# Cross attention's keys: one scaling pass, turned by VectorE squares and GpSimd DMAs; four small reorderings elsewhere

## The reference, cut to what matters

```
def memory_cross_attention(hn, mem, w_xq, w_xkv, g_mem, g_xq, g_xk, w_xo):
    q = (hn @ w_xq).reshape(B, T, 4, 256);  q = rmsnorm(q, g_xq)
    k, v = jnp.split(rmsnorm(mem, g_mem) @ w_xkv, 2, axis=-1)
    k = rmsnorm(k.reshape(B, M, 4, 256), g_xk)
    logits = jnp.einsum('bthd,bmhd->bhtm', q, k) * 256 ** -0.5
    p = jax.nn.softmax(logits, axis=-1)
    return jnp.einsum('bhtm,bmhd->bthd', p, v).reshape(B, T, 1024) @ w_xo
```

## Time and profile before

| | |
|---|---|
| median of three executions | 882.25 us |
| the profiled execution's own time | 883.71 us |
| its span, first to last instruction | 881.9 us |
| PE busy | 873.5 us (99%) |
| DVE busy | 601.1 us (68%) |
| ACT busy | 439.4 us (50%) |
| POOL busy | 183.2 us (21%) |
| mean granted TensorE clock | 0.998 |
| DMA | 154.67 MB, mean 175 GB/s |

### The profile page before, as it was taken

How to read it: one execution, slowest core, us unless ns; L and a number is a source line. 1 busy time by engine, 2 the same in 40 slices (tenths; PEclk the granted TensorE clock), 3 DMA queues, 4 the chain that set the end, 5 groups by cost and what they waited for, 6 DMA issues and landing times.

```text
span 881.9 us, 12721 instructions
## 1 busy us (share of the span) xinstructions
PE 873.5 (99%) x5023; PEld 751.7 (85%) x5023; DVE 601.1 (68%) x875; ACT 439.4 (50%) x613; POOL 183.2 (21%) x214
## 2 busy tenths in 40 slices
PE   9999999999999999999999999999999999999998
PEld 6897888888988999988888789888888888888886
DVE  5478988998696666745454948977785566665742
ACT  6365456864545555533344426546554544443531
POOL 0432234863110000000004222100100024444500
PEclk9999999999999999999999999999999999999999
DMA  8874542445146655655569765523542567775862
GB/s 297 200 258 144 191 144 87 132 129 166 48 139 195 193 191 190 190 191 191 190 212 258 201 165 192 189 98 118 170 142 79 164 199 218 219 220 160 254 218 72
DMA packets 87651, 154.67 MB, mean 175 GB/s; under 512 B 10528, under 2 KB 18512, under 8 KB 87472
## 3 DMA queue, kind: packets, MB, share of 16 engines
q1 hardware_dynamic: 80352, 144.55, 51.1%
q0 software_dynamic: 4720, 5.86, 3.7%
q10 hardware_dynamic: 2528, 3.56, 1.2%
HBM read 147.53 MB, written 1.44 MB: 169 GB/s over the span
## 4 chain that ended last, share of the span: by engine, by line
PE 92%; DVE 5%; DMA 1%; ACT 1%; issue 1%; SPq 0%; DVEq 0%; ACTq 0%
PE gemm L540 68%; PE gemm L1048 5%; PE mixbank L1048 5%; DVE w_lo L1872 2%; PE mixbank L603 1%; PE mixbank L702 1%; DMA raw<-in_w_in_dram 1%; PE mixbank L727 1%; PE mixbank L808 1%; PE mixbank L1213 1%; DVE mix L2010 1%; PE gemm L1241 1%; PE mixbank L713 1%; PE mixbank L750 1%; PE mixbank L902 0%
## 5 line engine op out<-in xcount | busy, mean ns | idle before, releaser
L1872 DVE TENSOR_TENSOR w_lo<-raw,w_hi 128x2048 fp32r<-128x2048 f32 (+3 forms) x132 | 288.0, 2189 | 180.3 <-ACT w_hi L1303 180.1
L1303 ACT ACTIVATE w_hi<-raw 128x2048 fp32r<-128x2048 f32 (+3 forms) x140 | 255.4, 1833 | 204.7 <-DMA raw<-in_w_in_dram 57.1
L540 PE MATMUL gemm<-w_hi,s_hi 128*128 128x512 f32 (+3 forms) x784 | 208.6, 386 | 0.6 <-ACT s_hi L1339 0.3
L540 PE MATMUL gemm<-w_lo,s_hi 128*128 128x512 f32 (+3 forms) x784 | 201.9, 378 | 1.2 <-DVE w_lo L1872 1.2
L540 PE MATMUL gemm<-w_hi,s_lo 128*128 128x512 f32 (+3 forms) x784 | 202.1, 378 | 0.0
L540 PEld LDWEIGHTS gemm<-w_lo,s_hi 128*128 128x128 f32 x784 | 142.6, 188 | 29.2 <-DVE w_lo L1872 2.1
L540 PEld LDWEIGHTS gemm<-w_hi,s_lo 128*128 128x128 f32 x784 | 143.2, 189 | 27.7
L540 PEld LDWEIGHTS gemm<-w_hi,s_hi 128*128 128x128 f32 x784 | 140.5, 189 | 26.0 <-issue 1.7
L2743 POOL TENSOR_TENSOR sm<-sm 128x2 f32<-128x2 f32 (+5 forms) x13 | 21.6, 1663 | 400.9 <-DVE sm L1933 296.5
L373 POOL DMA_DIRECT2D hid_moved<-hid_blocks x96 | 54.7, 578 | 72.4 <-DVE hid_blocks L2685 70.1
L2737 POOL TENSOR_TENSOR w_lo<-raw,w_hi 128x2048 fp32r<-128x2048 f32 x8 | 36.8, 4614 | 36.1 <-ACT w_hi L1303 36.1
(11 more groups left out here) (365 smaller groups left out, 1183.8 us busy)
## 6 DMA issues: line engine op xcount, KB each, us to landing
raw<-in_w_in_dram SPq DMA_DIRECT2D x40, 1024.0 KB, 5.2
raw<-in_w_mlp_up_dram SPq DMA_DIRECT2D x16, 1024.0 KB, 5.6
raw<-in_w_mlp_down_dram SPq DMA_DIRECT2D x16, 1024.0 KB, 5.1
raw<-in_w_gate_dram SPq DMA_DIRECT2D x10, 1024.0 KB, 5.3
raw<-in_w_up_dram SPq DMA_DIRECT2D x10, 1024.0 KB, 5.1
raw<-in_w_down_dram SPq DMA_DIRECT2D x10, 1024.0 KB, 5.4
raw<-in_w_out_dram SPq DMA_DIRECT2D x8, 1024.0 KB, 5.2
raw<-in_w_xkv_dram SPq DMA_DIRECT2D x8, 1024.0 KB, 5.1
```

What stands on the lines that cost most here:

```text
L540: return nc.tensor.matmul(G[b % 2][t][:, 0:width], lhs, rhs, start=kt == 0 and not (low_x or low_w), stop=kt == blk["kt"] - 1 and (low_x i ...
L1303: nc.scalar.activation(w_hi[:, n % SLOTS, 0:kn, 0:width], raw[:, n % SLOTS, 0:kn, 0:width], ACT.Copy)\
L1872: V.tensor_tensor(w_lo[:, s, 0:kn, 0:width], raw[:, s, 0:kn, 0:width], w_hi[:, s, 0:kn, 0:width].bitcast(F32), ALU.subtract)\
```

## The change

1. Keys. Each head's 256 columns are scaled by norm and gain in one instruction (`scalar_tensor_tensor`, 8 in all), placed between VectorE's two splits of block `B_XQ`. The keys are then turned by `turn_squares` behind `mean_squares(4)` and by 16 DMAs of `move` on GpSimd's queue into `X_MOVED`. TensorE's 16 transposes and the four copies go. `cross_logits` now waits for all 16 DMAs (`x_moved`) and reads `X_MOVED` in two runs of 128 columns.
2. Place (a): the three gate instructions go behind a later split. Place (b): TensorE issues `queries_back(2)` and `(3)` ahead of the second step's corners, and VectorE copies to `PS` ahead of one `turn_square`. Place (c): ACT issues the DMA of `WR` after the output of block `B_2 + 1`. Place (d): the memory rows are moved two DMAs at a time, over eight splits.

```diff
-        xkT = view(ar2, T0 + 2048, 8, SEQ)
+        X_BLOCKS = view(ar2, 12304, NT * D)
+        X_MOVED = view(ar2, T0 + 2048, NT * D)
...
                     if step == 1:
+                        if half == 0:
+                            for p in range(2, 4):
+                                queries_back(p)
                         pe.wait_ge(sem("inv_pc"), 2 + half + 1)
...
-            for p in range(2, 4):
-                queries_back(p)
             mm(B_GA, quarters=[2])
...
             mm(B_XQ, turned=28)
-            pe.wait_ge(sem("x_k"), 1)
-            cross_operands(range(4))
...
             def cross_logits(k):
+                pe.wait_ge(sem("x_moved"), 16 * 16)
...
-                        last = nc.tensor.matmul(M[k % 2][:, SEQ * j:SEQ * j + SEQ], xqT[:, 2 * h + e, P * t:P * t + P], xkT[:, 2 * h + e, :],
+                        o = M[k % 2][:, SEQ * j:SEQ * j + SEQ].rearrange("p (t n) -> p t n", n=P)
+                        last = nc.tensor.matmul(o, xqT[:, 2 * h + e, P * t:P * t + P], moved(X_MOVED, 2 * h + e), start=e == 0, stop=e == 1)
...
-            act.dma_start(WR, ret_w).then_inc(sem("ret_w_in"), 16)
             squares(2, x)
...
                 project(B_2 + k, P2R[:, 0, NCOL * k:NCOL * k + NCOL], rs2)
+                if k == 1:
+                    act.dma_start(WR, ret_w).then_inc(sem("ret_w_in"), 16)
...
-            V.tensor_copy(after_r[:, :], cst[:, C_AFTER:C_AFTER + P])
...
-            link(V.tensor_copy(gates_hi[:, :], GA_))
-            V.tensor_tensor(gates_lo[:, :], GA_, gates_hi[:, :].bitcast(F32), ALU.subtract).then_inc(sem("gdn_g"), 1)
             project(B_Q + 2, PQ[:, 1, NCOL * 2:NCOL * 3], RS[:, 1:2])
...
             begin(B_Q + 4)
+            V.tensor_copy(after_r[:, :], cst[:, C_AFTER:C_AFTER + P])
+            dve.wait_ge(sem("gdn_g"), 1)
+            link(V.tensor_copy(gates_hi[:, :], GA_))
+            V.tensor_tensor(gates_lo[:, :], GA_, gates_hi[:, :].bitcast(F32), ALU.subtract).then_inc(sem("gdn_g"), 1)
             select(range(4))
...
-            turn_square(1)
             for half in range(2):
                 dve.wait_ge(sem("inv_p"), 2 + 2 * half + 2)
                 V.tensor_copy(PS[96:128, 8 * half:8 * half + 8, 64:96], corner_bank(half, 1)[96:128]).then_inc(sem("inv_pd"), 1)
+            turn_square(1)
...
             residual(B_O2, 0)
-            begin(B_O2 + 1)
+            link(V.tensor_tensor(vec[:, V_XK:V_XK + 256], vec[:, V_XK:V_XK + 256], vec[:, V_XQ:V_XQ + 256], ALU.mult))
+            split(B_XQ, 0)
+            dve.wait_ge(sem("root"), root("xk"))
+            for t in range(NT):
+                for h in range(4):
+                    k = KV[:, t, 256 * h:256 * h + 256]
+                    ins = V.scalar_tensor_tensor(k, k, RNX[:, 4 * t + h:4 * t + h + 1], vec[:, V_XK:V_XK + 256], ALU.mult, ALU.mult)
+            link(ins)
+            split(B_XQ, 1)
             residual(B_O2 + 1, 1)
 
             turn_lo(NORMS["xattn"])
             mean_squares(4)
...
-                ins = V.tensor_tensor(kv[t], kv[t], spread(vec[:, V_XK:V_XK + 256], 1, 4), ALU.mult)
-            ins.then_inc(sem("x_k"), 1)
+            turn_squares(X_BLOCKS, KV).then_inc(sem("squares_turned"), 1)
...
-            for i, (b, c) in enumerate(((B_2, 1), (B_2 + 1, 1), (B_2 + 2, 0), (B_2 + 2, 1))):
+            for n in range(8):
-                pool.wait_ge(sem("split_hi"), blocks[b]["chunk0"] + c + 1)
-                move(pool, MEM, mem_blocks[:, :], "mem_moved", [i])
+                pool.wait_ge(sem("split_hi"), blocks[B_2 + 1]["chunk0"] + n)
+                move(pool, MEM, mem_blocks[:, :], "mem_moved", [n // 2], range(2 * (n % 2), 2 * (n % 2) + 2))
...
             norm_power(4)
+            pool.wait_ge(sem("squares_turned"), 3)
+            move(pool, X_MOVED, X_BLOCKS, "x_moved")
```

More of the change, by code:

```diff
@@ L366, in place_base, with move @@
             return eng.dma_start(dst[rows, :, rows], base_x[k, m].rearrange("n j i -> j n i"))
-        def move(eng, dst, src, name, bands=range(4)):
+        def move(eng, dst, src, name, bands=range(4), targets=range(4)):
             d, s = (v.rearrange("p (n j b) -> p n j b", j=4, b=32) for v in (dst, src))
             for i in bands:
-                for j in range(4):
+                for j in targets:
                     eng.dma_start(d[32 * j:32 * j + 32, :, i, :], s[32 * i:32 * i + 32, :, j, :]).then_inc(sem(name), 16)
@@ L1181, in cross_operands @@
                         pe.wait_ge(sem("att_exp"), X0 + 1)
[L1182 to L1186, removed]
+                    pe.wait_ge(sem("ev0"), B_XQ + 1 + (e - 4) // 2)
+                    pe.wait_ge(sem("ev1"), B_XQ + 1 + (e - 4) // 2)
                     for j in range(2):
@@ L1189, in cross_operands @@
                             c = P * (2 * (e % 4) + j)
-                            src = (KV if e < 4 else XQ)[:, t, c:c + P]
-                            last = nc.tensor.transpose(M[CROSS_BANK[e]][:, (2 * j + t) * P:(2 * j + t + 1) * P], src, ident)
+                            last = nc.tensor.transpose(M[CROSS_BANK[e]][:, (2 * j + t) * P:(2 * j + t + 1) * P], XQ[:, t, c:c + P], ident)
                     last.then_inc(sem("xT_pe"), 1)
             mm(B_XQ, turned=28)
-            pe.wait_ge(sem("x_k"), 1)
-            cross_operands(range(4))
             def cross_logits(k):
                 t, heads = WORK_X[k]
-                pe.wait_ge(sem("xT_act"), 3 if k < 2 else 4)
-                pe.wait_ge(sem("xT_dve"), 3 if k < 2 else 4)
+                pe.wait_ge(sem("x_moved"), 16 * 16)
+                pe.wait_ge(sem("xT_act"), 1 if k < 2 else 2)
+                pe.wait_ge(sem("xT_dve"), 1 if k < 2 else 2)
                 if k >= 2:
@@ L1212, in cross_logits @@
                     for e in range(2):
-                        last = nc.tensor.matmul(M[k % 2][:, SEQ * j:SEQ * j + SEQ], xqT[:, 2 * h + e, P * t:P * t + P], xkT[:, 2 * h + e, :],
-                                                start=e == 0, stop=e == 1)
+                        o = M[k % 2][:, SEQ * j:SEQ * j + SEQ].rearrange("p (t n) -> p t n", n=P)
+                        last = nc.tensor.matmul(o, xqT[:, 2 * h + e, P * t:P * t + P], moved(X_MOVED, 2 * h + e), start=e == 0, stop=e == 1)
                 last.then_inc(sem("att_logits"), 1)
@@ L1746, in cross_operand @@
             def cross_operand(e):
-                act.wait_ge(sem("xT_pe"), e + 1)
-                dst = (xkT if e < 4 else xqT)[:, 2 * (e % 4):2 * (e % 4) + 2, :]
+                act.wait_ge(sem("xT_pe"), e - 3)
+                dst = xqT[:, 2 * (e % 4):2 * (e % 4) + 2, :]
                 nc.scalar.activation(dst, M[CROSS_BANK[e]].rearrange("p (a b) -> p a b", a=2), ACT.Copy).then_inc(sem("xT_act"), 1)
@@ L1776, in _ @@
             act.wait_ge(sem("root_asked"), root("xk"))
-            cross_operand(0)
-            cross_operand(2)
             query_sums(0)
@@ L2424, in _ @@
                     dve.wait_ge(sem("mem_in"), 16)
-                    turn_squares(mem_blocks, mem_rows).then_inc(sem("mem_blocks"), 1)
+                    turn_squares(mem_blocks, mem_rows).then_inc(sem("squares_turned"), 1)
                 for t in range(NT):
@@ L2441, in _ @@
                     dve.wait_ge(sem("stat_ss"), 8)
-                    turn_squares(RET_BLOCKS, P2R).then_inc(sem("ret_blocks"), 1)
+                    turn_squares(RET_BLOCKS, P2R).then_inc(sem("squares_turned"), 1)
                 split(B_2 + k + 1, 1)
@@ L2589, in cross_operand @@
             def cross_operand(e):
-                dve.wait_ge(sem("xT_pe"), e + 1)
-                dst = (xkT if e < 4 else xqT)[:, 2 * (e % 4):2 * (e % 4) + 2, :]
+                dve.wait_ge(sem("xT_pe"), e - 3)
+                dst = xqT[:, 2 * (e % 4):2 * (e % 4) + 2, :]
                 V.tensor_copy(dst, M[CROSS_BANK[e]].rearrange("p (a b) -> p a b", a=2)).then_inc(sem("xT_dve"), 1)
@@ L2627, in _ @@
             project(B_XQ, XQ[:, 1, 0:NCOL], RS[:, 9:10])
-            cross_operand(1)
-            cross_operand(3)
             query_means(0)
@@ L2845, in _ @@
             norm_power(2)
-            pool.wait_ge(sem("mem_blocks"), 1)
+            pool.wait_ge(sem("squares_turned"), 1)
             for t in range(NT):
                 pool.wait_ge(sem(f"ev{t}"), B_2)
-            for i, (b, c) in enumerate(((B_2, 1), (B_2 + 1, 1), (B_2 + 2, 0), (B_2 + 2, 1))):
-                pool.wait_ge(sem("split_hi"), blocks[b]["chunk0"] + c + 1)
-                move(pool, MEM, mem_blocks[:, :], "mem_moved", [i])
-            pool.wait_ge(sem("ret_blocks"), 1)
+            for n in range(8):
+                pool.wait_ge(sem("split_hi"), blocks[B_2 + 1]["chunk0"] + n)
+                move(pool, MEM, mem_blocks[:, :], "mem_moved", [n // 2], range(2 * (n % 2), 2 * (n % 2) + 2))
+            pool.wait_ge(sem("squares_turned"), 2)
             for i, (b, c) in enumerate(((B_2 + 4, 0), (B_2 + 4, 1), (B_2 + 5, 0), (B_2 + 5, 1))):
```

1 line of the change is left out of this document (removed).

## The result

Four executions of the changed kernel took 888.36 to 890.01 us, median 889.12, against a median of 881.96 for four of the kernel before on the same chip. The ratio is 1.0077, 95% interval 1.0064 to 1.0089: slower, and outside the forecast's range (879.6 to 886.8). The profiled execution took 889.23 us, its span 887.2, 5.3 more than before.

What follows compares the result with a forecast made beforehand. TensorE, busy 873.5 of 881.9 us, was taken as the bound. The terms -1.75 + 0.1 + 4.6 + 1.7 - 0.2 - 1.5 - 1.0 gave +1.95 us: 885.7 profiled, 884.2 as median, range 879.6 to 886.8.

Steps and rivals of the forecast that it cites:

- Transposes, -1.75: TensorE's 16 transposes from 643.31 us go; it had not waited for them, so a clean 1.75 us is won.
- Residual, +0.1: The residual behind VectorE's second split, on which TensorE's next transposes wait, comes up to 0.2 us later; 0.1 taken.
- Start and issue of the moves: GpSimd's 16 moves start at 639.1 behind the squares and take 10.3 us, less what is won before.
- Landing: The last move lands 5.7 us after issue, at 654.4, so TensorE waits 4.6 us (1.6 to 7.3) before the logits.
- The end 8.4: Late end for the last move's landing: 8.4 us after issue, as one at 470.9, so 657.1.
- rival 3: Moves land late (8.4 us), or the clock falls at 219 as well: 885.1 to 887 us; chance 0.13.
- The clock, +1.7 (0 to 1.8): After the idle before the logits TensorE's clock falls to its lower level, costing 1.7 us.
- (a) -0.2: At 107.74 us, VectorE's three small instructions go behind the split TensorE awaited 0.21 us; 0.2 us won.
- (b) -1.5: At 217 us the 0.6 us wait and the clock's fall go, but ACT is late next; 1.5 us won.
- (c) and (d) -1.0: At 494 us the 1.01 us wait on VectorE's split goes, as its load lands earlier; 1.0 us won.
- Carrying over to the median, -1.46: The median lies 1.46 us under the profiled execution; carried over, 885.7 becomes 884.2 us.
- The remark on this in the sum: If runs without a profile lack the clock's fall at 219 us anyway, 0.9 us less is won there.

Runs made afterwards that it cites:

- e6_loads_held: The changed kernel, but SP issues the loads of w_xo only when all 16 moves have landed; one execution, 891.01 us.
- e1_reorder: The kernel before with only the four reorderings, the keys going their old way; median 880.22 us, ratio 0.9975.
- e7_fill6: The changed kernel with 6 matmuls that nobody reads in front of TensorE's wait for x_moved; median 887.95 us, ratio 1.0066.
- e2_keys: The kernel before with the keys' part of the change alone, no reordering; median 890.78 us, ratio 1.0100.
- e3_early: The changed kernel with the keys' squares right behind the scaling and all 16 moves ahead of norm_power(4); median 882.39 us, ratio 1.0001.

## Why the prediction was wrong, point by point

- **Transposes, -1.75:** right (2.73 to 4.49 us ahead, 1.76). **Residual, +0.1:** 0.17.
- **Start and issue of the moves:** right, 636.38 and 10.33 us for 16.
- **Landing, "I take 5.7", hence +4.6 of wait:** this is the step that failed. It was 8.0 and the wait 7.2. I took the landing from rows of other bursts by their number and size, and gave the loads in the same stretch one clause ("as there were around the hidden moves"). There were three chunks in that stretch and not two. And the hidden moves, from whose 5.3 us I reasoned, keep the engines 2.0 us in all, where these keep them 7.4: half the bytes, but little more than a quarter of the load. e6_loads_held shows that the last landing is 2.3 us with the loads held back, so the rest is what ran beside it. The end 8.4 stood in the range and in rival 3, whose mechanism (moves and loads hold each other up) is what happened, at its end of the range. I gave it 0.13, and its time, 885.1 to 887, is still too low, since the clock and the carrying over came on top.
- **The clock, +1.7 (0 to 1.8):** the mechanism was right and its size off, 2.67. The bound was taken from 3.4 us of low stretch at 219; here 5.3 us of work ran at half rate. After an idle of 4.5 us it was 4.6, and cost 2.3.
- **(a) -0.2:** 0.5. TensorE is 0.20 us behind at 106.66 and 0.31 ahead at 109.38, so "more than that isn't there to win" was wrong. The 0.20 was lost earlier and is not explained.
- **(b) -1.5:** 1.47 (0.42 to 1.89); ACT is late next, as said.
- **(c) and (d) -1.0:** 1.3 at 494 (1.60 ahead at 457.00, 2.88 at 492.48), less 0.3 for the idle at 456.19, which is not explained either. Loads of 452 to 482 us take 5.4 instead of 10.0 in the median.
- **Carrying over to the median, -1.46:** failed too. The profiled execution before lay 1.46 us above its median and is of the kind with the low clock at 219, which not every execution has; the two kinds are 1.8 us apart. Place (b) takes that away, and the changed kernel's profile (889.23) lies near its median (889.12). The remark on this in the sum priced it at 0.9.

The three sizes make up the miss: 2.6 of wait, 1.0 of clock, 1.35 of carrying over are 4.9, as from 884.2 to 889.1.

## What to carry to other kernels

When a transfer goes into a stretch that other transfers use, don't take its landing from another burst: add up how long each keeps the DMA engines (share of the queue times the stretch, here 0.46 us for a 64 KB move, 0.13 for a 32 KB one and 3.0 for a chunk of 1 MB) and see when the sum is worked off. Here 16.4 us from 635.3 on gives 651.7 at the earliest. The engines were full until 653.4, and the last move had landed at 654.1. Before you put a burst of DMAs ahead of a small instruction, look for every engine that waits for that instruction, not only for the reader of its value. And where one execution is profiled, ask which of its rows other executions lack before you carry a difference over to the median.

## What the hardware showed that I had not expected

- A 64 KB move from SBUF to SBUF costs the DMA engines 2.3 times what a load costs per byte (142 against 330 GB/s), one of 32 KB with the same 128-byte runs 1.3 times (260). A load of 1 MB beside the 64 KB ones takes 8.9 us instead of 5.1.
- A wait costs TensorE more than its idle: without the 0.21 us at 107.74 the rows behind it start 0.51 us sooner, without the 1.01 us at 494.33 1.28 us sooner. e1_reorder has the same two steps (0.64 to 1.15 us ahead, 2.71 to 3.98).
- The clock stayed at its upper level through an idle of 1.2 us (e6_loads_held), and fell in idles of 4.5, 5.0, 6.6 and 7.0 us (e7_fill6, e2_keys, e6_loads_held, the changed kernel). It also fell in e3_early, where the longest wait was 1.8 us with two of 0.2 ahead of it: the windows 645 to 648 and 648 to 651 us show a granted clock of 0.78 and 0.65.
- In the kernel before, the same instructions at 215 to 222 us let the clock fall in some executions and not in others: a profile shows one of the two.
- Open: in which executions the last move of e2_keys lands how late. The two groups by clock (0.996 and 0.992) differ by 4 us, more than the fall at 219 (1.8) explains, and only one execution has a trace. Open too: what makes a 64 KB move so much dearer than a 32 KB one.
